# MLP of a decoder layer: 512-wide products, the samples as a narrow fp32 stream, the up-projection by one level of Strassen's method, activations by way of DRAM

## The reference

```python
h = h + cross_attn(rmsnorm(h, p['g_cross']), mkv, p['w_cq'], p['w_co'])
u = jnp.square(jax.nn.relu(rmsnorm(h, p['g_mlp']) @ p['w_up']))
return h + u @ p['w_down']
```

## Time and profile before

| | us |
|---|---|
| median of 3 runs | 2272.22 (2265.78 to 2274.92) |
| profiled execution | 2280.15 |
| its span, first to last instruction | 2278.4 |
| PE busy | 2109.2 (93%) |
| DVE busy | 1046.3 (46%) |
| ACT busy | 524.2 (23%) |
| POOL busy | 114.7 (5%) |

### The profile page before, as it was taken

How to read it: one execution, slowest core, us unless ns; L and a number is a source line. 1 busy time by engine, 2 the same in 40 slices (tenths; PEclk the granted TensorE clock), 3 DMA queues, 4 the chain that set the end, 5 groups by cost and what they waited for, 6 DMA issues and landing times. The chain is left out here.

```text
span 2278.4 us, 39794 instructions
## 1 busy us (share of the span) xinstructions
PE 2109.2 (93%) x17420; PEld 1826.6 (80%) x17420; DVE 1046.3 (46%) x1270; ACT 524.2 (23%) x987; POOL 114.7 (5%) x143
## 2 busy tenths in 40 slices
PE   7999967789899789979999999789999999999998
PEld 7999954565456455548898898579999999999998
DVE  5222244645688678852222434775323323422424
ACT  4000004440444233321111223342101101101111
POOL 0000000001560011110000000000000000000000
PEclk9999978779899999999999999789999999999999
DMA  6113132020796589963111130301111111111112
GB/s 207 47 46 131 33 113 84 2 61 13 249 326 251 222 308 348 348 229 137 51 37 50 45 118 10 111 19 46 48 47 47 47 47 43 49 50 40 49 57 79
DMA packets 178908, 241.70 MB, mean 106 GB/s; under 512 B 27211, under 2 KB 165427, under 8 KB 173412
## 3 DMA queue, kind: packets, MB, share of 16 engines
q1 hardware_dynamic: 172792, 155.80, 22.0%
q0 software_dynamic: 5904, 83.95, 9.9%
q10 hardware_dynamic: 92, 0.20, 0.0%
HBM read 217.20 MB, written 66.72 MB: 125 GB/s over the span
## 5 line engine op out<-in xcount | busy, mean ns | idle before, releaser
L2536 PE MATMUL ps<-xn_hi,mlp_w_hi 128*128 128x344 f32 x768 | 163.3, 321 | 2.4 <-issue 1.8
L2536 PE MATMUL ps<-u_lo,mlp_w_hi 128*128 128x344 f32 x768 | 163.0, 320 | 0.0
L2536 PE MATMUL ps<-u_hi,mlp_w_hi 128*128 128x344 f32 x768 | 162.9, 320 | 0.0
L2536 PE MATMUL ps<-mlp_xn_lo,mlp_w_hi 128*128 128x344 f32 x768 | 162.9, 320 | 0.0
L2536 PE MATMUL ps<-u_hi,mlp_w_lo 128*128 128x344 f32 x768 | 162.1, 319 | 0.0
L2536 PE MATMUL ps<-xn_hi,mlp_w_lo 128*128 128x344 f32 x768 | 162.1, 319 | 0.0
L1288 PE MATMUL ps<-mla_rt,q_now 32*32 32x256 f32 x4608 | 144.9, 384 | 12.7 <-DVE mla_rt L1381 6.5
L1381 DVE STREAM_TRANSPOSE mla_rt<-qkvT 128x1536 f32<-128x1536 f32 x72 | 124.7, 1760 | 33.4 <-DMA qkvT<-in_cache_mla,page_rows 25.6
L1699 DVE TENSOR_TENSOR hT<-hT,ps 128x1032 f32<-128x1032 f32 x28 | 34.4, 1229 | 223.9 <-PE ps L2536 223.9
L2536 PE MATMUL ps<-xn_hi,gate_w_hi 128*128 128x344 f32 x576 | 128.1, 331 | 6.3 <-DVE gate_w_lo L2047 3.4
L1288 PEld LDWEIGHTS ps<-mla_rt,q_now 32*32 32x32 f32 x4608 | 85.9, 106 | 57.2 <-issue 31.8
(11 more groups left out here) (406 smaller groups left out, 3411.0 us busy)
## 6 DMA issues: line engine op xcount, KB each, us to landing
out_s_dsa_w<-in_cache_dsa_w SPq DMA_DIRECT2D x8, 4094.0 KB, 82.1
oaT<-in_w_up SPq DMA_DIRECT2D x32, 512.0 KB, 4.1
oaT<-in_w_down SPq DMA_DIRECT2D x32, 512.0 KB, 4.2
obT<-in_w_in SPq DMA_DIRECT2D x23, 512.0 KB
gate_w<-in_w_in SPq DMA_DIRECT2D x16, 512.0 KB, 4.1
out_s_dsa_w<-in_cache_dsa_w SPq DMA_DIRECT2D x8, 1022.0 KB, 17.4
s_kv_tile<-in_cache_dsa_w SPq DMA_DIRECT2D x12, 512.0 KB, 5.3
x_scr<-qkvT SPq DMA_DIRECT2D x1, 4128.0 KB, 13.2
```

Source lines behind the costliest of these rows:

```text
L2536: last = nc.tensor.matmul(out[:, t, 0:TC], w, x[:, k, t * TC:(t + 1) * TC], start=first, stop=stop)
```

## The change

The MLP is written anew; the rest of the kernel stays. The 8 samples are taken out of the wide products, so that the prompt has 1024 columns, two halves of 512 (`HT`).

*Up-projection.* The contraction is cut in two halves of 4 chunks (`KH`), the tokens in two halves of 512, and the hidden chunks in pairs (`NPAIR` = 16). The four blocks of a pair's result are made from seven block products instead of eight (P1 to P7): of weight blocks or sums of them (`weight_sum`) and activation blocks (`B11`, `B21`, `B22`) or sums of them (`T1` to `T4`, made once at the start). One block product is 12 matmuls of 512 columns (4 chunks x 3 parts). The seven are added up partly in PSUM (P6 onto P1, P7 onto the same, P3 onto P5), partly by copies of intermediate states (`snap`) and sums on DVE (`drain`). The weights' high and low parts go through a ring of 4 buffers (`wring`).

*Activations.* The two hidden chunks of a pair stand in `z`; DVE applies relu and 1/rms, ACT squares, and POOL stores each chunk (512 KB) to a DRAM tensor `u_scr`. For the down-projection POOL fetches them again, four at a time (`u_raw`); ACT and DVE split them.

*Down-projection.* Eight blocks (`NS`) of four hidden chunks; for each block all 8 output chunks, 24 matmuls of 512 columns each, added to `hT`.

*Samples.* They run as fp32 products (no split) with 128 columns of raw weights as the moving operand and 32 sample columns (8 used) as the stationary one, four at a time on four 32-column tiles of PE (`sample_quad`, `down_quad`); PE turns the results back.

*Other moves.* The squares of the first norm are summed by POOL, not DVE; the statistics products stand behind the third block product; the root stands in ACT's fourth step.

```diff
+    seq = [("P2", 0)]
+    for p in range(NPAIR):
+        seq += [("P1", p), ("P5", p), ("P6", p), ("P3", p), ("P7", p)]
+        if p + 1 < NPAIR:
+            seq.append(("P2", p + 1))
+        seq.append(("P4", p))
...
+    BANK = {"P2": lambda p: 0, "P1": a_bank, "P6": a_bank, "P7": a_bank, "P4": a_bank,
+            "P5": lambda p: 2, "P3": lambda p: 2}
+    OPERAND = {"P2": "B21", "P1": "B11", "P5": "T1", "P6": "T2", "P3": "B22", "P7": "T3", "P4": "T4"}
...
+        for p in range(NPAIR):
+            if p == 1:
+                sp.wait_ge(summed, KD - 1)
+            if p >= 2:
+                sp.wait_ge(lo_made, pos["P4", p - 2] + 1)
+                sp.wait_ge(smp_made, (p - 2) // 2 + 1)
+            sp.dma_start(rawp[p % 2], w_up[:, :, p * 2 * P:(p + 1) * 2 * P]).then_inc(raw_in[p % 2], 16)
...
+    def pool_work(pool):
+        def store(p, m):
+            pool.wait_ge(z_sq[m], p + 1)
+            pool.dma_start(u_scr[:, 2 * p + m, :], z[:, m, 0:SEQ]).then_inc(z_out[m], 16)
+
+        def fetch(s, k):
+            c = SL * s + k
+            pool.wait_ge(z_out[c % 2], 16 * (c // 2 + 1))
+            if s == 0:
+                pool.wait_ge(made, pos["P5", NPAIR - 1] + 1)
+            else:
...
+        for c in range(1, KD):
+            pool.wait_ge(squared, c + 1)
+            if c >= 2:
+                pool.wait_ge(summed, c - 1)
+            nc.gpsimd.tensor_tensor(ssum, ssum, sq[(c - 1) % 4], ALU.add).then_inc(summed, 1)
...
+        def twelve(bank, slot, name, first, chunkwise):
+            xh, xl = XB[name]
+            for k in range(KH):
+                if chunkwise:
+                    pe.wait_ge(x_low[name], k + 1)
+                for n, (w, x) in enumerate(((0, xh), (0, xl), (1, xh))):
+                    last = nc.tensor.matmul(ps[:, bank, :], wring[:, slot, w, k, :], x[:, k, :],
+                                            start=(first and k == 0 and n == 0), stop=(k == KH - 1 and n == 2),
+                                            skip_group_check=True)
+            return last
+
+        def sample_quad(q):
+            for s in range(2):
+                pe.wait_ge(*loaded(2 * q + s))
...
+            for k in range(KD):
+                for g in range(4):
+                    last = nc.tensor.matmul(ps[32 * g:32 * g + 32, 4, 0:P], xs[:, k, :],
+                                            rawp[g // 2][:, k, (g % 2) * P:(g % 2 + 1) * P], start=(k == 0),
+                                            stop=(k == KD - 1), tile_position=(0, 32 * g), skip_group_check=True)
+            last.then_inc(smp_made, 1)
...
+        for i, (kind, p) in enumerate(seq):
+            name = OPERAND[kind]
+            pe.wait_ge(lo_made, i + 1)
...
+            if kind == "P6":
+                pe.wait_ge(c11, p + 1)
+            if kind == "P3":
+                pe.wait_ge(snap5, p + 1)
+            if kind == "P7":
+                pe.wait_ge(snap2, p + 1)
+            if kind == "P4":
+                pe.wait_ge(c22, p + 1)
+            twelve(BANK[kind](p), i % WS, name, kind in ("P2", "P1", "P5"), i == 0).then_inc(made, 1)
+            if i == 2:
+                pe.wait_ge(summed, KD - 1)
+                for t in range(NT):
+                    if t == 2:
+                        pe.wait_ge(rooted, 1)
+                    nc.tensor.matmul(ps[:, 6 + t % 2, 0:TC], ones[:], ssum[:, t * TC:(t + 1) * TC],
+                                     start=True, stop=True).then_inc(spread, 1)
+            if i in quads:
+                sample_quad(quads[i])
+            if i - 2 in quads:
+                turn_fold(quads[i - 2])
...
+        for d in range(ND):
+            s, c = d // KD, d % KD
+            i = N_UP + d
+            xh, xl = UB[s % 2]
...
+                if c == 0:
+                    pe.wait_ge(u_lo, SL * s + k + 1)
+                for n, (w, x) in enumerate(((0, xh), (0, xl), (1, xh))):
+                    for t in range(2):
+                        last = nc.tensor.matmul(ps[:, 2 * (d % 2) + t, :], wring[:, i % WS, w, k, :],
+                                                x[:, k, t * HT:(t + 1) * HT], start=(k == 0 and n == 0),
+                                                stop=(k == SL - 1 and n == 2))
+            last.then_inc(made, 1)
+            if c % 4 == 1:
+                down_quad(s, c // 4)
...
+        for i in range(N_ALL + 1):
+            kind, p = seq[i - 1] if 1 <= i <= N_UP else (None, 0)
+            if kind == "P5":
+                act.wait_ge(made, i)
+                if p:
+                    act.wait_ge(c22, p)
+                nc.scalar.activation(snap[:, 1], ps[:, 2, :], ACT.Copy).then_inc(snap5, 1)
+            if kind == "P6":
+                act.wait_ge(made, i)
+                if p:
+                    act.wait_ge(c12, p)
+                nc.scalar.activation(snap[:, 0], ps[:, a_bank(p), :], ACT.Copy).then_inc(snap2, 1)
+            if i + 2 < N_ALL:
+                upper(i + 2)
...
+            if i == 2:
+                act.wait_ge(t_made["T3"], KH)
+                nc.scalar.activation(XB["T3"][0], x_tmp[:, 0], ACT.Copy).then_inc(x_up["T3"], 1)
+            if i == 3:
+                for t in range(NT):
+                    act.wait_ge(spread, t + 1)
+                    nc.scalar.activation(rstd[:, t * TC:(t + 1) * TC], ps[:, 6 + t % 2, 0:TC], ACT.Sqrt,
+                                         bias=eps[:, 0:1], scale=1.0 / D).then_inc(rooted, 1)
+            if i == 4:
+                act.wait_ge(t_made["T4"], KH)
+                act.wait_ge(x_low["T3"], 1)
+                nc.scalar.activation(XB["T4"][0], x_tmp[:, 1], ACT.Copy).then_inc(x_up["T4"], 1)
+            if i in u_steps:
+                s, k = u_steps[i]
+                act.wait_ge(u_in[k], 16 * (s + 1))
+                act.wait_ge(made, u_free(s))
+                nc.scalar.activation(UB[s % 2][0][:, k], u_raw[:, k], ACT.Copy).then_inc(u_hi, 1)
+            kind, p = seq[i - 2] if 2 <= i <= N_UP + 1 else (None, 0)
+            if kind == "P2":
+                act.wait_ge(made, i - 1)
+                if p:
+                    act.wait_ge(z_out[0], 16 * p)
+                else:
+                    act.wait_ge(summed, KD - 1)
+                nc.scalar.activation(z[:, 0, 0:HT], ps[:, 0, :], ACT.Copy).then_inc(snap0, 1)
+            if kind == "P3":
+                square_z(p, 0)
+            if kind == "P4":
+                square_z(p, 1)
...
+            if kind == "P5":
+                dve.wait_ge(*loaded(p))
+                if p:
+                    dve.wait_ge(lo_made, pos["P3", p - 1] + 1)
+                ins_ = (s_tmp[:, 0], a21, a22, ALU.add)
+            elif kind == "P6":
+                dve.wait_ge(lo_made, pos["P5", p] + 1)
+                ins_ = (s_tmp[:, 0], s_tmp[:, 0], a11, ALU.subtract)
+            elif kind == "P3":
+                dve.wait_ge(lo_made, pos["P6", p] + 1)
+                ins_ = (s_tmp[:, 0], s_tmp[:, 0], a12, ALU.subtract)
...
+                if p:
+                    dve.wait_ge(lo_made, pos["P7", p - 1] + 1)
+                ins_ = (s_tmp[:, 1], a11, a21, ALU.subtract)
+            nc.vector.tensor_tensor(*ins_).then_inc(w_sum, 1)
+
+        def lower(i):
+            dve.wait_ge(hi_made, i + 1)
+            nc.vector.tensor_tensor(wring[:, i % WS, 1], source(i), wring[:, i % WS, 0].bitcast(F32),
+                                    ALU.subtract).then_inc(lo_made, 1)
...
+        def drain(i):
+            if i >= N_UP:
+                d = i - N_UP
+                c = d % KD
+                dve.wait_ge(made, i + 1)
+                h = hT[:, c, 0:SEQ].rearrange("p (a n) -> p a n", a=2)
+                nc.vector.tensor_tensor(h, h, ps[:, 2 * (d % 2):2 * (d % 2) + 2, :], ALU.add).then_inc(drained, 1)
+                return
+            kind, p = seq[i]
+            a = a_bank(p)
+            if kind == "P1":
+                dve.wait_ge(made, i + 1)
+                dve.wait_ge(snap0, p + 1)
+                nc.vector.tensor_tensor(z[:, 0, 0:HT], ps[:, a, :], z[:, 0, 0:HT], ALU.add).then_inc(c11, 1)
+            if kind == "P3":
+                dve.wait_ge(made, i + 1)
+                dve.wait_ge(snap2, p + 1)
+                nc.vector.tensor_tensor(z[:, 0, HT:SEQ], snap[:, 0], ps[:, 2, :], ALU.subtract).then_inc(c12, 1)
+                dve.wait_ge(c12, p + 1)
+                if p == 0:
+                    dve.wait_ge(inverted, NT)
+                nc.vector.scalar_tensor_tensor(out=z[:, 0, 0:SEQ], in0=z[:, 0, 0:SEQ], scalar=0.0, in1=rstd[:, 0:SEQ],
+                                               op0=ALU.max, op1=ALU.mult).then_inc(z_r[0], 1)
+            if kind == "P7":
+                dve.wait_ge(made, i + 1)
+                dve.wait_ge(snap5, p + 1)
+                if p:
+                    dve.wait_ge(z_out[1], 16 * p)
+                nc.vector.tensor_tensor(z[:, 1, HT:SEQ], ps[:, a, :], snap[:, 1], ALU.subtract).then_inc(c22, 1)
+            if kind == "P4":
+                dve.wait_ge(made, i + 1)
```

(71 more changed lines are left out.)

484 lines of the change are left out of this document (322 added, 162 removed).

## The result

The changed kernel takes 2284.11 us (median of 9 runs), the one before in the same runs 2273.67: a ratio of 1.0049, 95% interval 1.0032 to 1.0065. That is 10 us slower. Forecast was 2220, 2.3% faster, with a range up to 2278. Of the rivals, the one that ends nearest is the rate of 2.18 columns a ns (2275), but that alone does not reach the time either.

The account below looks back on a forecast made before the run. PE bounds the MLP (734.4 us) by number and pace of matmuls. After: products 621.8 + samples 33 + statistics 2.3 + start 18 + switch 5 = 680.1, tail +2: 52.3 less than 2272.2, 2220; range 2204 to 2278 (own 2204 to 2238).

Parts of the forecast that it names:

- the rate of 2.18 columns a ns: Rival: MLP products stream at a fixed rate, 235.0 ns per 512 columns; 55 us more, 2275, no change; chance 0.17.
- The pace: MLP products: a 512-wide one takes 215.9 ns, its surcharge mostly hidden; 2880 of them cost 621.8 us.
- the 429 ns of an fp32 record: Existing 512-column fp32 products, two records each: 2.6 ns over 426.7, the surcharge carried over to give 215.9 ns.
- Samples: Separate fp32 sample products in the up and down phases: 28.2 us plus 24 changes of array shape at 0.2, 33 us.
- Start: Before the first P4: added DVE and ACT work makes PE 18 us late, bounds 8 to 30.
- the walk: Step through three engine queues at the start: PE idle 1538.5 to 1547 on ACT's root, P4 near 1563.4, not 1546.3.
- Switch: Between up- and down-projection: last P4 about 4 us late, plus 0.8 for P7's drain, 5 us.
- Tail: Before the y loop: fold, transposes, small adds, square and reduce add 2 us to the 20.15 after the last product.
- The fixed surcharge: Rival: each MLP product carries a fixed 14.6 ns, so 512 columns cost 227.9; 34.6 us more, 2255; chance 0.17.
- The doubled samples: Rival: tiled sample products cost twice the price, 61 us; 28 us more, 2248; chance 0.09.
- the store as a price for each pair: Rival: the DRAM store delays ACT's copy into z0 and P6 behind it, 15 pairs; up to 2323, slower; chance 0.07.
- the slack of 8.3 us: Up-projection, per pair: 3.2 products' time for the store to land before the next P6; about 5 us expected, no wait.

Follow-up runs that it names:

- the 512-wide kernel before: The kernel before with its MLP products 512 wide, two in place of three, sample tokens left out of the MLP, no Strassen: 2258.17 us, ratio 0.9928.
- the 344-wide down-products: The changed kernel with down-products as three of 344 columns, samples inside, in place of two of 512 and a narrow stream: 2271.58 us, ratio 0.9975.

## Why the prediction was wrong

From the first wco product to the end the sum had 52.3 us less; the profiles have 8.9 more. Of these 61 us, by the prediction's own terms:

- **The pace, +46.** The failing step: "something takes about 157 ns beside each product and shows only when the product is shorter than that". It was read off one fact, that the surcharge is gone at 1.2 GHz. A ceiling of 2.2 columns a ns explains that fact as well, since 1.2 stays below it, and the prediction said so among its rivals. A 256-wide product in 117.7 ns shows that nothing of 157 ns stands beside it. 2880 x (232.0 - 215.9) = 46.4. The other leg was weaker still: the 429 ns of an fp32 record are a stream at 1.2 columns a ns, so they lie below the ceiling and say nothing on a stream at 2.4. Both rows that spoke for 216 were slow streams; the fast stream among the rows, 344 columns in 157.9 ns, spoke for 228 to 235, and 232.0 was measured.
- **Samples, +3.** 8 x 2.09 + 16 x 1.21 = 36 against 33. The step of four records was right (0.109 us against 0.107); the 24 changes of shape cost 0.34 us each, there and back, where the estimate was 0.2.
- **Start, +9.** Taken from the trace after: 764.3 us from the first wco product to the last residual, less 668.1 for products, 25.2 for the output projection as before, 36.1 and 0.7 for samples and their folds, 2.8 for statistics, 4.4 for the switch, leave 27 against 18. PE's waits are 20.2 of them, near the forecast, in part by luck: the wait for the first product's operands (6.6, some 5 in the walk) and the one on the root (7.2, 8.5 in the walk) came; the 6.4 in the output projection were not in the walk, which has all of PE's idle time behind it, and its last 3.5 before P4 did not come. The walk took DVE's durations from the earlier trace rows, where POOL was idle, and left the output projection at full pace. The rest is the clock: 18.6 us of work at 0.5 against 5.4 before cost some 6 us. The prediction named that for its upper bound of 30 and left it out of the 18. DVE and POOL holding each other up is about half: with POOL's additions cut short some 13 of the 27 us came back, waits and clock together. The root's wait could be taken away without a gain.
- **Switch, -1.** PE waits 2.8 there, for DVE's drain behind the splits, as forecast; the clock is 0.5 for 3.4 us after it, which costs 1.6 more. That is 4.4 against 5.
- **Folds and statistics, +1.** The sum had nothing for the folds of the up-projection (0.7) and 2.3 for statistics that took 2.8.
- **Tail, +2.** 24.30 against 20.15 + 2.

That is 46 + 3 + 9 - 1 + 1 + 2 = 60; the 61 is missed by rounding. Strassen's step itself delivered: 192 products fewer than the 3072 of the 512-wide kernel before, 192 x 0.232 = 45 us, and the width 15 (727.6 - 3072 x 0.232). Of these 60 us the stream and its folds took 37; the start, switch, statistics and tail took 32 more than before, which leaves the 9 us lost.

Of the rivals, the rate comes nearest (232.0 where it had 235.0, and 363 us for the 344-wide down-products), though the excess is not quite in proportion to the width. The fixed surcharge misses (227.9; 27 us for the 512-wide kernel before, where 14 to 16 came). The doubled samples are refuted (36 us against 61). So is the store as a price for each pair: it landed in 3.0 us (32 stores), and PE never waits behind it. That ACT would not wait for it was wrong (26.1 us in eight pairs), but the slack of 8.3 us covered waits of at most 3.9. DVE's 52% never became the bound beyond the first pair and the switch.

## What to carry to other kernels

A surcharge that vanishes at the lower clock may be hidden work or a ceiling on a rate; a block of products at two or three widths tells them apart in one run, and a sum that hangs on it should wait for that. Idle time ahead of PE can be paid twice: here PE's clock fell to 0.5 late in each of its three longer waits. Before moving elementwise work to GpSimd to relieve VectorE, look whether VectorE is running at the same time: here the additions of each took 0.4 to 1.1 us longer beside the other's, and the relief became the delay. A few stray columns can be cheapest inside the wide products: here a round width made a second stream that cost six times what they had.
